# Filling TensorE's waits at stage changes with products of constants (two transformer blocks, 256 tokens, one core)

## What is computed

```python
for layer in range(2):                        # first_block
    h = rmsnorm(x, g[layer, 0])
    m = rwkv7_time_mix(h, ...) if layer == 0 else mla(h, ...)
    x = x + rmsnorm(m, g[layer, 1])
    f = conv_ffn(rmsnorm(x, g[layer, 2]), ...)        # 1024 -> 2 x 2816 -> 1024
    x = x + rmsnorm(f, g[layer, 3])
for i in range(2):                            # second_block
    h = rms_norm(x, norm_mix[i])
    x = x + (diff_attention(h, ...) if i == 0 else dsa_attention(h, ...))
    x = x + sq_relu_mlp(rms_norm(x, norm_mlp[i]), w1[i], w2[i])   # 1024 -> 4096 -> 1024
```

## Time and profile before

| | |
|---|---|
| runs | 1512.64, 1514.64, 1514.97 us (median 1514.64) |
| the profiled execution | 1508.34 us |
| its span | 1506.5 us |
| mean granted TensorE clock | 0.971 |
| PE busy | 1409.9 us, 94% of the span |
| DVE, ACT busy | 900.7 and 626.5 us, 60% and 42% |

### The profile page before, as it was taken

How to read it: one execution, slowest core, us unless ns; L and a number is a source line. 1 busy time by engine, 2 the same in 40 slices (tenths; PEclk the granted TensorE clock), 3 DMA queues, 4 the chain that set the end, 5 groups by cost and what they waited for, 6 DMA issues and landing times.

```text
span 1506.5 us, 21947 instructions
## 1 busy us (share of the span) xinstructions
PE 1409.9 (94%) x8660; PEld 1228.1 (82%) x8660; DVE 900.7 (60%) x1579; ACT 626.5 (42%) x953; POOL 61.1 (4%) x45
## 2 busy tenths in 40 slices
PE   5999999989999897989999898889999998999998
PEld 3885998789999656889999677679999767889997
DVE  6277456667676513577676566665555667475553
ACT  2332221253343326653433455653433457454331
POOL 0002000000000001100000002000000023000000
PEclk9999998999999899999999899899999999999999
DMA  6423101145654133265555243075642213376420
GB/s 219 171 79 112 57 2 57 57 168 197 202 187 143 43 119 112 65 233 178 189 175 176 72 169 135 34 285 204 223 177 103 99 51 111 112 280 224 179 100 28
DMA packets 110796, 208.11 MB, mean 138 GB/s; under 512 B 3808, under 2 KB 53088, under 8 KB 110208
## 3 DMA queue, kind: packets, MB, share of 16 engines
q1 hardware_dynamic: 110720, 207.06, 39.3%
HBM read 205.99 MB, written 1.05 MB: 137 GB/s over the span
## 4 chain that ended last, share of the span: by engine, by line
PE 85%; DVE 7%; ACT 5%; issue 2%; DMA 0%; SPq 0%; DVEq 0%; ACTq 0%
PE ps L819 19%; PE ps L739 12%; PE ps L805 10%; PE ps L800 10%; PE ps L795 9%; PE ps L1034 4%; PE ps L717 3%; PE ps L855 3%; PE ps L866 2%; ACT Ah L1403 1%; PE ps L1157 1%; PE ps L1266 1%; PE ps L1145 1%; DVE arena L2367 1%; PE ps L692 1%
## 5 line engine op out<-in xcount | busy, mean ns | idle before, releaser
L1413 ACT CAST Ah<-ringA 128x2048 fp32r<-128x2048 f32 x76 | 145.1, 1909 | 281.3 <-PE ps L805 266.9
L1979 DVE TENSOR_TENSOR Al<-ringA,Ah 128x2048 fp32r<-128x2048 f32 x76 | 174.2, 2292 | 85.5 <-ACT Ah L1413 85.2
L795 PE MATMUL ps<-hTh,Ah 128*128 128x256 f32 x1216 | 169.7, 281 | 5.3 <-DVE hTl L1964 5.1
L800 PE MATMUL ps<-hTl,Ah 128*128 128x256 f32 x1216 | 170.8, 283 | 0.4 <-DVE hTl L1964 0.3
L805 PE MATMUL ps<-hTh,Al 128*128 128x256 f32 x1216 | 169.4, 282 | 0.0
L795 PEld LDWEIGHTS ps<-hTh,Ah 128*128 128x128 f32 x1216 | 159.3, 188 | 11.7 <-issue 5.6
L1986 DVE TENSOR_TENSOR Bl<-ringB,Bh 128x1024 fp32r<-128x1024 f32 (+1 forms) x76 | 127.0, 1671 | 53.8 <-ACT Bh L1422 53.8
L800 PEld LDWEIGHTS ps<-hTl,Ah 128*128 128x128 f32 x1216 | 156.4, 190 | 0.8 <-DVE hTl L1964 0.8
L805 PEld LDWEIGHTS ps<-hTh,Al 128*128 128x128 f32 x1216 | 155.2, 190 | 0.0
L1422 ACT CAST Bh<-ringB 128x1024 fp32r<-128x1024 f32 (+1 forms) x76 | 107.3, 1412 | 111.8 <-PE ps L819 108.6
L819 PE MATMUL ps<-Bh,hidh 128*128 128x512 f32 x432 | 134.3, 392 | 4.5 <-issue 3.0
(11 more groups left out here) (354 smaller groups left out, 2042.2 us busy)
## 6 DMA issues: line engine op xcount, KB each, us to landing
ringA<-in_ffn_w_in SPq DMA_DIRECT2D x44, 1024.0 KB, 6.8
ringA<-in_mlp_w SPq DMA_DIRECT2D x32, 1024.0 KB, 7.6
ringB<-in_mlp_w SPq DMA_DIRECT2D x32, 1024.0 KB, 6.8
ringB<-in_ffn_w_out SPq DMA_DIRECT2D x44, 512.0 KB, 4.1
ringA<-in_diff_w_in SPq DMA_DIRECT2D x12, 1024.0 KB, 6.8
ringA<-in_dsa_w_in SPq DMA_DIRECT2D x8, 1024.0 KB, 6.3
ringA<-in_w_k SPq DMA_DIRECT2D x4, 1024.0 KB, 8.6
ringA<-in_w_r SPq DMA_DIRECT2D x4, 1024.0 KB, 6.2
```

What stands on the lines that cost most here:

```text
L795: mm(o, Ah[:, half, k * T + j * P:k * T + j * P + P], hTh[:, k, :], start=(k == 0), stop=False)
L800: mm(o, Ah[:, half, k * T + j * P:k * T + j * P + P], hTl[:, k, :], start=False, stop=False)
L1413: nc.scalar.copy(a_split(w, Ah, half), a_half(w, ap, half)).then_inc(ah_rdy, 1)
L1979: V.tensor_tensor(a_split(w, Al, half), a_half(w, (a_at[w] + par) % 2, half), a_split(w, Ah, half).bitcast(F32), ALU.subtract).then_inc(al ...
```

## The change

A new helper `keep(n, b)` issues `n` plain float32 products of the 128x128 identity with 256 columns of the table of constants, into bank `b` of PSUM, which nothing uses at that point. They wait for nothing and nobody waits for them. 105 such products are placed at 25 points of PE's program, nearly all at a change of stage; no other engine's program is touched.

```diff
                         if name in LATE:
                             if k == 0:
+                                if t and name in ("n1", "n2", "n3"):
+                                    keep(1, 0)
                                 pe.wait_ge(x_done, 2 * (NI[name] - 1) + t + 1)
...
+            def keep(n, b):
+
+                for _ in range(n):
+                    mm(ps[:, b, 0:T], ident, con[:, 0:T], start=True, stop=True)
...
             pe.wait_ge(con_in, 32)
             turn16("n0")
+            keep(9, 7)
...
                 if name in BEFORE:
                     need(u, *BEFORE[name])
+                    if (u, name) in ((2, "y1"), (2, "U"), (3, "U"), (2, "Y")):
+                        keep(1, lane_bank(u, name))
...
             turn16("o0")
+            keep(3, 3)
             out_proj(0)
+            keep(7, 7)
             turn16("nf0")
             ffn("ffn0", 1)
...
                 for h in range(heads):
+                    if diff and h == 0:
+                        keep(6, 1)
+                    if diff and h == heads - 1:
+                        keep(3, 3)
                     turn(h)
...
+            keep(5, 7)
             turn16("n1")
+            keep(5, 0)
             wait_hT("n1")
...
+            keep(10, 0)
             pe.wait_ge(job_out, J["qk1"][0])
             pe.wait_ge(pre["src"], 1)
             turn_blocks(J["qk1"][0], ...)
+            keep(2, 0)
             pe.wait_ge(job_out, J["qk1"][0] + 16)
             attend(0, ...)
             turn16("o1")
             out_proj(1)
+            keep(7, 7)
             turn16("nf1")
+            keep(1, 0)
             ffn("ffn1", 1)
+            keep(7, 7)
             turn16("n2")
             for s in range(6):
                 split_jobs(a_at["din"] + s, ...)
                 if s == 3:
                     pe.wait_ge(pre["dq"], 1)
                     turn_blocks(J["q2"][0], ...)
+                    keep(7, 1)
...
             attend(1, ...)
+            keep(9, 3)
             turn16("o2")
             out_proj(2)
             turn16("nm0")
+            keep(4, 0)
             ffn("mlp0", 2)
...
             turn16("n3")
+            keep(2, 0)
             sin_jobs(0)
...
             sin_jobs(4)
+            keep(7, job_bank(J["k3"][0]))
             pe.wait_ge(pre["src"], 4)
             turn_blocks(J["k3"][0], ...)
...
             turn16("nm1")
+            keep(4, 0)
             ffn("mlp1", 2)
```

## The result

The changed kernel takes 1501.11 us (median of 5 runs, 1500.88 to 1505.95) against 1514.97 us (5 runs, 1512.64 to 1515.1): a ratio of 0.992 with a 95% interval of 0.9904 to 0.9937, or 12 us less (the medians are 13.9 apart). The forecast was 1506.3, the right way but 5 us short: 1501.1 lies in the whole range (1499.5 to 1512.5), but under the forecast's own (1502.5 to 1510), where rival 2 was put with a chance of 0.13. The profiled execution took 1503.19 us (span 1501.4, clock 0.989), which is only 5.1 us less span than the profiled one of before. Most of what follows is about that gap between 5, 8 and 12.

The account below looks back on a forecast made before the run. PE's chain was taken as the bound, with half clock behind its waits as avoidable loss. Gains of 11.3 us less 3.0 for misplaced products gave 8.3, so 1514.64 - 8.3 = 1506.3 us (own range 1502.5 to 1510, whole range 1499.5 to 1512.5).

Parts of the forecast that it names:

- rival 2: Timed executions lose more to the clock than the profiled one: 1503, or 1500 if all; chance 0.13 beyond 1502.5.
- k3: Stage with 16 transposes at half clock: 1.9 us to gain, less the pace of four ACT copies, so 1.6.
- n0: Norm wait of 7.1 us, nine products: at most 2.3 us, taken as 1.2 because 3.2 us stay empty.
- misplaced, units 2 and 3: Four single products in RWKV, one pair before the waits of unit 4: 1.7 us of delay on the chain.
- o0: Short wait behind which the clock doesn't fall in the trace: 0, a few tenths in executions where it would.
- n2: Norm wait with 5.16 us at 0.50 behind it: 2.6 at most, halved to 1.3 for waits left inside the turning.
- misplaced, turn(7): Three products in differential attention, one head after the wait before turn(6): taken as 1.3 us of delay.
- o2: 4.56 us at 0.50 give 2.3, less 0.6 of PE waiting for ACT's evictions: 1.7 us gained.
- nm0: Wait before mlp0: gains nothing, since a faster start of mlp0 makes the later wait before L819 (2.44 us) longer.
- Rival 1: Small waits that stay, inside n1, n2, nf0 and at n0's end, bring the clock down as before: 1510.8; chance 0.14.
- Rival 3: Transposes don't count as work for the clock, so q and k, k3 and parts of n1, o2 go: 1510.1; chance 0.03.
- rivals 4 and 5: Constant products don't hold the clock: 1517.6, chance 0.08; identity's weight load isn't hidden, 0.72 us per product: 1520.9, chance 0.04.

Follow-up runs that it names:

- first execution: Kernel before, unchanged: the profiled execution that the prediction was made from, 1508.34 us, span 1506.5 us.
- the ninth experiment: Kernel before, unchanged, profiled once more: 1513.82 us, span 1512.0 us, clock 0.965.
- first experiment: Changed kernel without the seven misplaced products (four at units 2 and 3 of the recurrence, three before turn(7)): 1498.50 us, ratio 0.9911 to the kernel before.
- the third experiment: Changed kernel with the seven misplaced products moved to the waits at units 4 and 5 and before turn(6): 1496.05 us, ratio 0.9893 to the kernel before.
- the sixth: Changed kernel with only the second block's kept products, from n2 on, and without the seven misplaced ones: 1507.23 us, ratio 0.9964 to the kernel before.
- all waits filled: The third experiment's kernel with more products in the rests of n0, n1, n2, nf0, nf1 and mlp0: 1492.09 us, ratio 0.9867 to the kernel before.
- the fourth experiment: Changed kernel with each kept product replaced by four transposes of the identity: 1503.33 us, ratio 0.9943 to the kernel before.

## Why the prediction was right, and where it was not

Matching the same instruction in the traces of before and after gives what each place brought. Start times of the first instruction behind each place were subtracted (k3, for example: 1262.74 against 1257.60 us for the first scores behind it, -5.14, after -3.59 in front of it). Gains are positive, in us:

| place | forecast | first execution | another (the ninth experiment) |
|---|---|---|---|
| n0 | 1.2 | 0.5 | 1.6 |
| near 150 to 160 us | - | -1.5 | 0 |
| misplaced, units 2 and 3 | -1.7 | -1.7 | -1.7 |
| units 4 and 5 | - | -1.5 | -1.4 |
| o0 | 0 | 0 | 0.7 |
| nf0 and nf1 | 0.4 | 0.35 | 0 |
| n1 | 2.0 | 2.1 | 2.9 |
| q and k | 1.0 | 1.3 | 1.7 |
| n2 | 1.3 | 2.7 | 2.9 |
| q2 | 1.7 | 1.6 | 1.6 |
| turn(0) | 0.4 | 0.45 | 0.2 |
| misplaced, turn(7) | -1.3 | 0.0 | -0.2 |
| o2 | 1.7 | 1.1 | 1.5 |
| nm0, to L819 | 0 | -1.9 | -1.7 |
| k3 | 1.6 | 1.6 | 2.6 |
| span | 8.3 | 5.1 | 10.6 |

- **The bound and the mechanism** were right: PE's chain, the price of 0.50 against 1.00, the kept product's 0.43 us, the events that end the waits unchanged. q2, n1, q and k, k3 and turn(0) came within 0.3 us of their terms against the first execution. n0 and o2 were put too high by 0.7 and 0.6. At n0 nine products are enough in some executions and not in others: of six traces with nine, three have a stretch at 0.50 behind them and gain some 0.6 us, and three have none and gain 2.3.
- **The two misplaced groups** were right in place. The four cost the forecast 1.7 us where they stand, and by the traces some 1.5 more at units 4 and 5 (first experiment), which I had not counted. The three at turn(7) were put at their whole 1.3 and cost 0.6 (first experiment), and the table shows none of it: before, the clock was 0.50 behind turn(6), which after it is not, and that gain of about the same size I hadn't counted.
- **n2 was mis-sized**, 1.3 for 2.7: the step that failed is that the clock may fall in the rests of the wait (1.13 and 1.34 us) all the same. In the changed kernel's trace it didn't; in the third experiment's it did, for 3.4 us from 842 us on (its filling is the same there), and in the sixth's for 6.8. So the doubt was right in kind for two of the seven traces with one product between the halves, and the gain was 2.6 to 2.7 in the other five.
- **nm0 failed.** "A faster start of mlp0 makes that wait longer" was right: 3.70 for 2.44 us. That the longer wait would bring the clock down behind itself I didn't see. Instructions of L826 then run at 0.50, and the place costs 1.9 us. Eight products there took back 1.1 of it (all waits filled). I also passed over a stretch at 0.50 at the start of mlp0 in the trace of before, from 996.5 to 999.9 us, behind nm0's own wait of 2.1 us:

  ```profile
  995.53:999.91 4.38, 4.38 (x24) 4.38 (x25) 4.38 (x7) 4.29 (x6) 0.00 (x0) 0.61 1.01 414
  ```

  With the four products of nm0 it is gone and these products start 0.9 us earlier, but the wait before L826 swallows that, as forecast.
- **o0 and the other short waits** were set to 0 because this trace showed no fall there. Other executions do, and the experiment without them puts them at 3 to 4.5 us in timed runs, with intervals that just touch.
- **The step from the profiled execution to the median** is what made the forecast 5 us short. I carried the difference of 6.3 us over as a constant. It is not one: the profiled execution had 87 us at 0.50 and two others 106, and the kept products remove the added 19 as well. Against one of those two the change is worth 10.6 us of span instead of 5.1. The changed kernel's own profiled execution is 2.1 us above its median besides. So two errors go against each other: between the profiled executions I promised too much (8.3 for 5.1), and between the medians too little (8.3 for 12 to 14). This was rival 2, at 1503 with a chance of 0.13; 1501.1 is between its two cases.

Rival 1 (the small rests undo it) was wrong at n1 in every trace with its products; at n2 it came true in two of seven and at n0 in part in three of six. Rival 3 (transposes don't count) is refuted by the fourth experiment, rivals 4 and 5 are refuted by the clock and by the 3.18 us of fourteen instructions.

Open: why the clock falls earlier at units 4 and 5 behind the four misplaced products. That it does goes with them in all ten traces compared in the first experiment, and not with the execution; the mechanism is not shown. Nor is the 1.5 us near 150 to 160 us explained by anything in the change; it is absent against the other execution, so it belongs to the execution.

## What to carry to other kernels

A wait on an engine that sets the pace has a second price, the clock behind it, and work that nobody needs can buy that off, if it ends in front of the event. Check each insertion against the idle time in the trace at that very instruction: one pair or one head off, and it is pure delay of its own length. Ask also which wait gets longer once the stage in front is faster, and fill that one too. And when the effect depends on the moment, one profiled execution is a sample: take two or three before carrying its sum to a median, and fill short waits in which it happened to show nothing.

## What the runs showed of the hardware

The clock fell with PE hardly idle, in two places. In the recurrence PE is busy for 22.10 of 24.43 us in the kernel before, with 64- and 128-column products and single waits under 1 us, and the granted clock there is 0.72; four products of 256 columns more, and it is 1.00 (third experiment). Near 150 us PE is busy throughout with 32 instructions on two columns each (L980), and the clock is at 0.50 behind them in every trace, that with all waits filled too, where it is the only stretch before the end: the page's share of busy time doesn't tell of this.

The same kernel's time moves by 6 us between executions (1508.7 to 1514.9), and in the three that were profiled the stretches at 0.50 differ with it. The total length at 0.50 doesn't fix the time: spans of 1507.0 and of 1510.2 us both have a mean clock of 0.971. With the waits filled the four runs lie within 2 us.
